# Branch C's queries and keys turned by DMA in two-byte halves instead of by TensorE

## The reference, cut to what matters

```python
def latent_attention(c_q, c_kv, c_kr, positions, cq_g, w_uq, ckv_g, w_ukv, qn_g, kn_g):
    q = (rms_norm(c_q, cq_g) @ w_uq).reshape(b, s, MLA_HEADS, MLA_QK)       # 128 + 64 columns a head
    kv = (rms_norm(c_kv, ckv_g) @ w_ukv).reshape(b, s, MLA_HEADS, MLA_NOPE + MLA_V)
    k_nope, v = kv[..., :MLA_NOPE], kv[..., MLA_NOPE:]
    k = jnp.concatenate([k_nope, broadcast(c_kr)], axis=-1)
    q, k = rms_norm(q, qn_g), rms_norm(k, kn_g)
    q = concatenate([q[..., :MLA_NOPE], apply_rope(q[..., MLA_NOPE:], positions)])
    k = concatenate([k[..., :MLA_NOPE], apply_rope(k[..., MLA_NOPE:], positions)])
    ...
    sc = jnp.einsum('bqhd,bkhd->bhqk', qi, kf) * scale
    w = jax.nn.softmax(jnp.where(mask, sc, NEG_INF), axis=-1)
    return jnp.einsum('bhqk,bkhd->bqhd', w, vf)
```

## Time and profile before

| what | value |
|---|---|
| median of 3 runs | 1358.57 us |
| the profiled execution's own time | 1358.55 us |
| its span | 1356.8 us |
| TensorE (PE) busy | 1350.7 us, 6401 matmuls |
| GpSimd (POOL) busy | 606.1 us |
| VectorE (DVE) busy | 699.5 us |
| ScalarE (ACT) busy | 560.5 us |
| DMA | 126.32 MB, mean 93 GB/s |

### The profile page before, as it was taken

The page is one execution under the profiler, slowest core; times in us unless marked ns, Lnnn a source line. Parts: engine busy times, 40 slices in busy tenths (PEclk is TensorE's granted clock), DMA queues, the critical chain, the costliest instruction groups (busy, mean ns, idle before and its releaser), DMA issues.

```text
span 1356.8 us, 16150 instructions
## 1 busy us (share of the span) xinstructions
PE 1350.7 (100%) x6401; PEld 1136.3 (84%) x6401; DVE 699.5 (52%) x1065; ACT 560.5 (41%) x870; POOL 606.1 (45%) x455
## 2 busy tenths in 40 slices
PE   9999999999999999999999999999999999999998
PEld 8788888888888888888888888888888888888887
DVE  7996445144553223265779955441445432343743
ACT  6365454255552222224444554443555322222242
POOL 3444252444434445445565542334333444544543
PEclk9999999999999999999999999999999999999999
DMA  7322222222222333323333222223222333333332
GB/s 209 92 86 94 63 79 74 90 86 85 87 79 93 93 100 102 109 93 96 99 108 94 85 94 63 78 75 97 78 79 81 90 95 104 97 93 109 100 101 95
DMA packets 68268, 126.32 MB, mean 93 GB/s; under 512 B 9040, under 2 KB 37984, under 8 KB 68192
## 3 DMA queue, kind: packets, MB, share of 16 engines
q1 hardware_dynamic: 66960, 124.72, 30.2%
q10 hardware_dynamic: 1232, 0.55, 0.1%
HBM read 123.15 MB, written 2.10 MB: 92 GB/s over the span
## 4 chain that ended last, share of the span: by engine, by line
PE 98%; DVE 1%; ACT 0%; issue 0%; DVEq 0%
PE ps L491 31%; PE ps L493 31%; PE ps L492 31%; PE ps L764 1%; PE ps L699 1%; PE ps L800 1%; PE ps L686 1%; PE ps L541 1%; PE ps L551 0%; DVE n_t L1453 0%; PE ps L556 0%; DVE h_lo L1336 0%; PE ps L582 0%; DVE r_b L1448 0%; PE ps L618 0%
## 5 line engine op out<-in xcount | busy, mean ns | idle before, releaser
L464 POOL TENSOR_TENSOR w_lo<-w_raw,w_hi 128x512 fp32r<-128x512 f32 x222 | 304.4, 1371 | 724.4 <-ACT w_hi L971 724.3
L491 PE MATMUL ps<-h_hi,w_hi 128*128 128x512 f32 (+1 forms) x1160 | 452.6, 390 | 1.0 <-DVE h_lo L1336 1.0
L493 PE MATMUL ps<-h_hi,w_lo 128*128 128x512 f32 (+1 forms) x1160 | 450.2, 388 | 0.0
L492 PE MATMUL ps<-h_lo,w_hi 128*128 128x512 f32 (+1 forms) x1160 | 449.9, 388 | 0.0
L971 ACT ACTIVATE w_hi<-w_raw 128x1024 fp32r<-128x1024 f32 x227 | 238.6, 1054 | 172.5 <-PE ps L493 166.5
L466 POOL TENSOR_TENSOR w_lo<-w_raw,w_hi 128x512 fp32r<-128x512 f32 x222 | 303.7, 1368 | 0.0
L491 PEld LDWEIGHTS ps<-h_hi,w_hi 128*128 128x128 f32 x1160 | 217.9, 188 | 46.6 <-DVE h_lo L1336 2.6
L493 PEld LDWEIGHTS ps<-h_hi,w_lo 128*128 128x128 f32 x1160 | 217.8, 188 | 45.1
L492 PEld LDWEIGHTS ps<-h_lo,w_hi 128*128 128x128 f32 x1160 | 217.9, 188 | 43.3
L1771 DVE SCALAR_TENSOR_TENSOR m_part<-th,ps 128x512 f32<-128x512 f32 x48 | 33.0, 687 | 237.9 <-PE ps L493 237.7
L1196 ACT ACTIVATE th<-ps 128x512 f32<-128x512 f32 x48 | 28.7, 597 | 183.5 <-PE ps L493 183.5
(11 more groups left out here) (329 smaller groups left out, 1992.2 us busy)
## 6 DMA issues: line engine op xcount, KB each, us to landing
w_raw<-w_in SPq DMA_DIRECT2D x180, 512.0 KB, 3.5
w_raw<-w_in SPq DMA_DIRECT2D x92, 128.0 KB, 2.5
w_raw<-w_in SPq DMA_DIRECT2D x36, 256.0 KB, 3.0
x<-x_in SPq DMA_DIRECT2D x8, 256.0 KB, 4.1
w_raw<-w_in SPq DMA_DIRECT2D x32, 64.0 KB, 2.0
out_x<-x SPq DMA_DIRECT2D x7, 256.0 KB, 3.7
p_raw<-p_in SPq DMA_DIRECT2D x2, 512.0 KB, 4.4
w_raw<-w_in ACTq DMA_DIRECT2D x4, 128.0 KB, 3.0
```

The source lines that it names most:

```text
L464: pool.tensor_tensor(w_lo_t[s][:, 0:4, :], w_raw_t[s][:, 0:4, :], w_hi_t[s][:, 0:4, :].bitcast(F32), ALU.subtract)
L491: pe.matmul(o, a_hi, b_hi, start=first, stop=False, skip_group_check=skip)
L492: pe.matmul(o, a_hi, b_lo, start=False, stop=False, skip_group_check=skip)
L493: return pe.matmul(o, a_lo, b_hi, start=False, stop=last, skip_group_check=skip)
```

## The change

TensorE's 24 transposes of a pair are gone. Instead, ScalarE copies each of the six tiles, read as 1024 two-byte numbers a partition, into two planes (all the low halves, then all the high halves), by `split`. SyncE turns each with one DMA transpose (`turn`), placed in its program ahead of the load of `yb1` or `yb3` (three tiles of the queries) and ahead of the load of `gb3` or `gb7` (three tiles of the keys). GpSimd puts the turned halves of the queries together again, in its program ahead of the low part of `gb3` or `gb7`; VectorE does that for the keys (`merge_halves`), between `branch_b(d)` and `branch_b(d+1)`. A key tile's DMA waits until GpSimd has put together the query tile with which it shares a semaphore. The high and low parts are then made from SBUF and no longer from PSUM.

```diff
--- before
+++ after
@@ -213,8 +214,11 @@
             *[(n, [SEQ], F32R) for n in ("kr_hi", "kr_lo", "qr_hi", "qr_lo")])
         k_sq, q_sq = plan(36, 46, ("k_sq", [TB, PAIR, P], F32), ("q_sq", [TB, PAIR, QK], F32))
         k_tok, q_tok, k_rot, q_rot = plan(
-            60, 72, ("k_tok", [TB, PAIR, P], F32), ("q_tok", [TB, PAIR, P], F32),
+            60, 72, ("k_tok", [PAIR, TB, P], F32), ("q_tok", [PAIR, TB, P], F32),
             ("k_rot", [TB, PAIR, 2, HALF], F32), ("q_rot", [TB, PAIR, 2, HALF], F32))
+        k_half, k_turned, q_half, q_turned, kr_half, kr_turned, qr_half, qr_turned = plan(
+            36, 60, *[(n, [PAIR, SEQ], F32) for n in ("k_half", "k_turned", "q_half", "q_turned")],
+            *[(n, [SEQ], F32) for n in ("kr_half", "kr_turned", "qr_half", "qr_turned")])
         prob, pt_hi, pt_lo, sz_c, th_b, tmp = plan(
             60, 83, ("prob", [TRI], F32), ("pt_hi", [TRI], F32R), ("pt_lo", [TRI], F32R), ("sz_c", [SEQ], F32),
             ("th_b", [2, SEQ], F32), ("tmp", [SEQ], F32))
@@ -282,7 +286,8 @@
 
         k_ready, k_squared, q_squared, q_taken, qk_var, qk_root, k_made, q_rotated = sems(
             "k_ready k_squared q_squared q_taken qk_var qk_root k_made q_rotated")
-        t_ready, t_hi_made, t_made = sems("t_ready t_hi_made t_made")
+        t_split, q_merged, k_merged, t_hi_made, t_made = sems("t_split q_merged k_merged t_hi_made t_made")
+        t_turned = [sem(f"t_turned{b}") for b in range(3)]
         s_ready, s_max, exp_made, p_made, pt_ready, pt_hi_made, pt_made, oc_ready, oc_gated, oc_hi_made, act_c_made = sems(
             "s_ready s_max exp_made p_made pt_ready pt_hi_made pt_made oc_ready oc_gated oc_hi_made act_c_made")
         gb_tanh, yb_ready, yb_taken, cz_tanh, cz_taken = sems("gb_tanh yb_ready yb_taken cz_tanh cz_taken")
@@ -313,6 +318,24 @@
         def by_head(t, block):
 
             return t.rearrange("p (h t c) -> p h t c", h=G, t=TB)[:, :, block, :]
+
+        def halves(t):
+
+            return t.bitcast(U16).rearrange("p (s u) -> p u s", u=2)
+
+        def planes(t):
+
+            return t.bitcast(U16).rearrange("p (u s) -> p u s", u=2)
+
+        TURNED = ((q_tok[:, 0], q_half[:, 0, :], q_turned[:, 0, :]), (q_tok[:, 1], q_half[:, 1, :], q_turned[:, 1, :]),
+                  (q_rot[:], qr_half[:], qr_turned[:]),
+                  (k_tok[:, 0], k_half[:, 0, :], k_turned[:, 0, :]), (k_tok[:, 1], k_half[:, 1, :], k_turned[:, 1, :]),
+                  (k_rot[:], kr_half[:], kr_turned[:]))
+
+        def flat_tok(b):
+
+            t = TURNED[b][0]
+            return t.rearrange("p t h a c -> p (t h a c)") if b in (2, 5) else t.rearrange("p t c -> p (t c)")
 
         def tile(t, i, n=SEQ):
 
@@ -396,6 +419,16 @@
                 for to, part in gathered(l, name):
                     sync.dma_start(to, part).then_inc(raw_loaded[c % RING], 16)
 
+            def turn(lp, first):
+
+                for b in range(first, first + 3):
+                    sync.wait_ge(t_split, after(lp * 6 + b))
+                    if b > 2:
+                        sync.wait_ge(q_merged, after(lp * 3 + b - 3))
+                    _, half, turned = TURNED[b]
+                    sync.dma_start_transpose(turned.bitcast(U16).rearrange("p (j s) -> p j s", j=2 * TB),
+                                             half.bitcast(U16)).then_inc(t_turned[b % 3], 16)
+
             def load_x(d):
                 sync.dma_start(tile(x, d), x_in[:, d * SEQ:(d + 1) * SEQ]).then_inc(x_loaded[d], 16)
 
@@ -429,6 +462,8 @@
                     if name == "wo0":
                         sync.wait_ge(act_a_made, after(l * G + G - 1))
                         sync.dma_start(p_raw[:], p_in[l]).then_inc(p_loaded, 16)
+                    if name in ("yb1", "gb3", "yb3", "gb7"):
+                        turn(l * 2 + (name in ("yb3", "gb7")), 0 if name.startswith("yb") else 3)
                     if l or not (name.startswith("lat") or name == "av0"):
                         load(l, name)
             for d in range(KD - 1):
@@ -449,6 +484,11 @@
                 for name in ORDER:
                     c = number(l, name)
                     s, n = c % RING, width(name)
+                    if name in ("gb3", "gb7"):
+                        lp = l * 2 + (name == "gb7")
+                        for b in range(3):
+                            pool.wait_ge(t_turned[b], 16 * after(lp * 2))
+                            pool.tensor_copy(halves(flat_tok(b)), planes(TURNED[b][2])).then_inc(q_merged, 1)
                     if 0 < c < RING:
 
                         continue
@@ -747,22 +787,6 @@
                 gate_b(l, d + 1, fill, gb_tanh, l * KD + d)
                 branch_b(l, d + 1, fill + 1, yb_taken, l * KD + d)
 
-                pe.wait_ge(k_made, after(lp))
-                pe.wait_ge(q_taken, after(lp))
-                pe.wait_ge(q_rotated, after(lp))
-                for b, t_of in enumerate((lambda t: k_tok[:, t, 0, :], lambda t: k_tok[:, t, 1, :],
-                                          lambda t: k_rot[:, t], lambda t: q_tok[:, t, 0, :], lambda t: q_rot[:, t],
-                                          lambda t: q_tok[:, t, 1, :])):
-                    if p == 0 and b == 4:
-                        pe.wait_ge(gb_tanh, after(l * KD + d + 1))
-                    if p == 0 and b == 5:
-                        pe.wait_ge(yb_taken, after(l * KD + d + 1))
-                    for t in range(TB):
-                        i = t_of(t)
-                        if b in (2, 4):
-                            i = i.rearrange("p h a c -> p (h a c)")
-                        last = pe.transpose(ps[:, b * 512 + t * P:b * 512 + (t + 1) * P], i, ident[:])
-                    last.then_inc(t_ready, 1)
                 gate_b(l, d + 2, 6, gb_tanh, l * KD + d + 1)
                 branch_b(l, d + 2, 7, yb_taken, l * KD + d + 1)
 
@@ -1143,6 +1167,10 @@
             def pair_c(l, p):
                 d, head, n, lp = 4 * p, PAIR * p, l * G + PAIR * p, l * 2 + p
                 kq, kb, fill = f"kq{p}", K_BANK[p], 10 - K_BANK[p]
+
+                def split(b):
+                    act.activation(planes(TURNED[b][1]), halves(flat_tok(b)), ACT.Copy).then_inc(t_split, 1)
+
                 act.wait_ge(k_ready, after(lp))
                 for b in range(2):
                     act.activation(k_sq[:, 2 * b:2 * b + 2].rearrange("p t h c -> p (t h c)"), bank(kb + b),
@@ -1153,20 +1181,28 @@
                                    ACT.Square).then_inc(q_squared, 1)
                 act.wait_ge(krr_made, after(l))
                 for t in range(TB):
-                    last = act.activation(q_tok[:, t], bank(t, PAIR * QK).rearrange("p (h c) -> p h c", h=PAIR)[:, :, 0:P],
+                    last = act.activation(q_tok[:, :, t, :], bank(t, PAIR * QK).rearrange("p (h c) -> p h c", h=PAIR)[:, :, 0:P],
                                           ACT.Copy)
                 last.then_inc(q_taken, 1)
                 weights_up_to(l, kq, 3)
                 act.wait_ge(qk_var, after(lp))
                 act.activation(sm("qk_root"), sm("qk_sum"), ACT.Sqrt, bias=eps[:], scale=1.0 / QK).then_inc(qk_root, 1)
+                act.wait_ge(q_taken, after(lp))
+                split(0)
+                split(1)
+                act.wait_ge(q_rotated, after(lp))
+                split(2)
                 gate_b(l, d, fill)
                 weights_up_to(l, kq, 4)
+                act.wait_ge(k_made, after(lp))
+                for b in (3, 4, 5):
+                    split(b)
                 gate_b(l, d + 1, fill)
                 weights_up_to(l, kq, 5)
-                for b, (o, gain) in enumerate(((kn_hi[:, 0], "kn"), (kn_hi[:, 1], "kn"), (kr_hi[:], None),
-                                               (qn_hi[:, 0], "qn"), (qr_hi[:], None), (qn_hi[:, 1], "qn"))):
-                    act.wait_ge(t_ready, after(lp * 6 + b))
-                    act.activation(o, bank(b), ACT.Copy, scale=col(l, gain) if gain else 1.0).then_inc(t_hi_made, 1)
+                for b, (o, gain) in enumerate(((qn_hi[:, 0], "qn"), (qn_hi[:, 1], "qn"), (qr_hi[:], None),
+                                               (kn_hi[:, 0], "kn"), (kn_hi[:, 1], "kn"), (kr_hi[:], None))):
+                    act.wait_ge(q_merged if b < 3 else k_merged, after(lp * 3 + b % 3))
+                    act.activation(o, flat_tok(b), ACT.Copy, scale=col(l, gain) if gain else 1.0).then_inc(t_hi_made, 1)
                 weights_up_to(l, kq, 6)
                 gate_b(l, d + 2, 6)
                 weights_up_to(l, kq, 7)
@@ -1673,22 +1709,33 @@
                 dve.tensor_scalar(sm("rq"), sm("qk_inv", 0, 8), Q_SCALE_C, None, ALU.mult)
                 dve.tensor_scalar(sm("neg_rq"), sm("qk_inv", 0, 8), -Q_SCALE_C, None, ALU.mult)
                 for b in range(2):
-                    dve.tensor_tensor(k_tok[:, 2 * b:2 * b + 2].rearrange("p t h c -> p (t h) c"),
-                                      bank(kb + b).rearrange("p (u c) -> p u c", u=4),
```

(30 more changed lines are left out.)

## The result

| | before | after |
|---|---|---|
| median of the device time, us | 1359.08 (1358.22 to 1361.79, 4 runs) | 1389.81 (1388.25 to 1391.84, 4 runs) |
| ratio | | 1.0225, 95% interval 1.0209 to 1.0242 |
| the profiled execution's time / span, us | 1358.55 / 1356.8 | 1391.09 / 1389.3 |
| TensorE's matmuls | 6401 | 6305 |

The change makes the kernel slower by 2.25%; 1394 was forecast, in a range of 1369 to 1425. The profiled execution is one of the longer ones of four, 1.3 us over their median.

A forecast was written before the change was run, and what follows sets the result against it. TensorE, busy 1350.7 of 1356.8 us, was taken to bound the kernel. 1358.55 - 10.5 (transposes) + 9.3 (first wait) + 29 (second wait) + 7.2 (clock) = 1393.6, say 1394 us; range 1369 to 1425.

The forecast's parts named there:

- The transposes: On TensorE, the 24 transposes removed from each pair, 2.62 us of the chain four times: -10.5 us.
- The first wait: TensorE ahead of gb(d+1) waits for the first tanh, delayed by ScalarE's three query copies: +9.3 us in all.
- The second wait: TensorE ahead of yb(d+2) waits for yb_taken behind merges and turning: 7.2 us a pair, +29 us in all.
- M: Time of one GpSimd merge of a query tile: taken as 1.7 us, between 1.28 and 2.56.
- T: Time for the turning DMA of the last key tile to land: taken as 3.5 us, at most 8.0.
- C: Time of VectorE's merge of the last key tile: taken as 1.1 us, between 0.84 and 1.78.
- the formula: TensorE's wait ahead of yb(d+2) in each pair: 3M + T + C - 2.48 us.
- The clock: After the wait ahead of yb(d+2), TensorE's matmuls may start at half pace: 1.8 us a pair, +7 us.
- What was to cost nothing: Loads held behind turnings on SyncE and VectorE's six low parts: no cost, scores waiting at most some tenths of a us.
- the rival of slow turning: T beyond 8.0, or query turnings delaying yb1's load and GpSimd; with T at 11 about 1435 us; chance 10%.
- the merges not quick enough: Rival of quick merges and a steady clock: wait under 3.9 us a pair, about 1365 us; chance 4%.
- The one on the other side: Rival: turned tiles ready in time, no wait at yb_taken, time falls to 1357 to 1348 us; chance 3%.

The follow-up runs named there:

- experiment 2: Changed kernel with GpSimd's three query merges ahead of yb1's low part (yb3's in the second pair) instead of behind it: 1368.28 us, ratio 1.0075.
- experiment 6: Changed kernel with the edits of experiments 1, 2 and 3, all six turnings behind yb1's load and SyncE not waiting for GpSimd's merges: 1357.31 us, ratio 0.9988.
- experiment 7: Changed kernel with only the key tiles' turnings freed from GpSimd's merges; the query merges stay behind yb1's low part: 1388.99 us, ratio 1.0217.
- experiment 3: Changed kernel with ScalarE's three query splits behind the first tanh instead of ahead of it: 1389.81 us, ratio 1.0229.
- experiment 8: Experiment 6's kernel with VectorE merging the query tiles too, and making each low part ahead of a key copy: 1347.81 us, ratio 0.9918 to the kernel before.
- experiment 1: Changed kernel with branch_b(d+1) ahead of the three key merges on VectorE: 1387.16 us, ratio 1.0212.
- experiment 4: Changed kernel with 20 more matmuls, their result unread, on TensorE ahead of its wait for yb_taken: 1387.22 us, ratio 1.0208.

## Why the prediction was right

**The mechanism** was as forecast in each step: a wait at the first tanh, a wait for `yb_taken` ahead of yb(d+2) in all four pairs with the merges, the turning and VectorE's queue in its chain, and a lower clock behind it.

**The transposes**: -10.5 forecast, -10.2 measured: the forecast took a record's duration (2.62), but between the starts lie 2.54 us.

**The first wait**: +9.3 forecast, +9.7 measured. The splits take 2.9 us (1.99 for two, 1.04 for the third).

**The second wait**: 7.2 a pair forecast, 5.3 measured. The term was oversized by its three prices: M is 1.25 between starts, not 1.7; T 3.2, not 3.5; C 0.63 between starts, not 1.1. By them the formula gives 3.75 + 3.2 + 0.63 - 2.48 = 5.1, and SyncE's 0.3 us to the issue, which it lacked, makes 5.4. The formula follows the last key tile. The profile's chain goes by the first key tile's turning and the three copies and three low parts of VectorE behind it. The two are equally long to some 0.1 us: GpSimd and SyncE pass a tile on every 1.3 us, and VectorE needs as long for a copy and a low part (141.24, 142.61, 143.90). So the counting of elements times operands overrated GpSimd's copy (two bytes, one operand), which costs about what its low part costs. A turning takes 3.2 us here and a plain load of 256 KB also 3.2; the rule of the Trainium skill (Advanced Engine Details and Errata, X-Bar Transpose) that turning DMAs are as fast as others agrees with that.

**The clock**: +7 forecast, +7.7 behind the second wait. Its 1.8 a pair was the middle of 0 and 3.6, with no row to price it, so its closeness is luck. A lower clock behind the first, shorter wait stood among the signs, but the sum had no term for it: +3.6 in the profiled execution. The two mistakes (-8 for the second wait, +4 here) offset each other in part, and that too is luck: without it 1394 would not be only 4 us off.

**What was to cost nothing** cost nothing in this kernel: the low parts' new source in SBUF took no longer (0.74, 0.68), since GpSimd was idle at that time. The rule by which GpSimd slows beside a VectorE instruction with two SBUF operands was given 0.9 us a pair on the side of GpSimd's merges, and did not act here. In experiments 2, 6 and 7, where the two engines work together, it is the larger on VectorE's side, 1 us an instruction, and it strikes the two-byte copies too, which have one SBUF operand. And the load of yb1 behind the query turnings was called free: it is, only because TensorE is already late. In experiment 3 ScalarE waits 8.4 us for it in all, and the longer second wait (+10.3) with a slower yb(d+2) behind it leaves nothing measurable of what the other edit gains; the rival of slow turning had this path, and it needs no slow turning.

**The rivals**: turning was not slow, and the merges not quick enough. The working of the slow one does not add up (1361 + 60 + 12 is 1433, and its 1361 comes from no row or sum); the forecast does not use it. The one on the other side, that the time falls if the tiles are ready in time, came true in experiment 8: its 1348 is what was measured (1347.8), once order, semaphores and engines were changed.

## What to carry to other kernels

Work taken off a fully busy engine is a gain only if each result that it made is still there when that engine asks, and in an in-order program the place of a new instruction decides that more than its price: here turning by DMA costs 31 us in one arrangement of order, semaphores and engines and gains 11 in another. After mending one wait, look for the next: experiments 3 and 7 mended a real one and gained nothing. Where VectorE and GpSimd both work in SBUF at a critical moment, try to give the work to one of them; here that came with a change of order, and some 2.5 of the 3.5 us won in a pair were instructions that took their usual time again.

## What the runs showed that I had not expected

After a wait of TensorE of 1.95 to 2.74 us the clock fell in some pairs and not in others (gb(d+1) at 7.2 instead of 5.5 us in one pair of experiments 1 and 2, in two of the kernel after, in all four of experiments 4 and 7). Each kernel has one trace, so how this differs between executions of one kernel is seen only in each run's mean granted clock: in experiment 7 it is 0.990 in the run of 1385.58 us and 0.986 in the three of 1388.8 to 1389.4. That the clock makes the spread of 3.6 us of the kernel after (0.988 to 0.991) fits but was not tested, and the kernel before, which has no such wait, also spread by 3.6 in four runs. A two-byte copy of 1024 elements is slowed from 0.74 to up to 1.87 us on VectorE beside a copy or a low part of GpSimd, which itself loses 0.4 to 0.5.
